# The loads of a decoder step's first ten microseconds dealt out anew over three queues, with four warm-up matmuls fewer

## What is computed

```python
h = RMSNorm(x)                        # x * rsqrt(mean(x*x) + eps) * attn_norm_w
[xin | Bg | Cg | q | k | v | g_conv | g_attn] = h @ w_in          # 1024 x 6400
y_conv = Bg * causal_depthwise_conv3(Cg * xin)
y_attn = sliding_window_attention(RMSNorm(q), RMSNorm(k), v)      # window 128, T5 bias, sinks
x = x + w_out(sigmoid(g_conv) * y_conv + sigmoid(g_attn) * y_attn)
x = x + MoE(RMSNorm(x))               # top 4 of 32 experts: 1024 -> 2 x 1024 -> 1024
```

## Time and profile before

| | |
|---|---|
| median of 3 runs | 1148.07 us (1147.94 to 1150.03) |
| the profiled execution: span from its first to its last instruction | 1145.4 us |
| TensorE busy | 1097.6 us, 96% of the span |
| mean granted TensorE clock | 0.993 |
| DVE, ACT, POOL busy | 38%, 16%, 8% |
| read from memory | 439.78 MB, 386 GB/s over the span |

### The profile page before, as it was taken

How to read it: one execution, slowest core, us unless ns; L and a number is a source line. 1 busy time by engine, 2 the same in 40 slices (tenths; PEclk the granted TensorE clock), 3 DMA queues, 4 the chain that set the end, 5 groups by cost and what they waited for, 6 DMA issues and landing times.

```text
span 1145.4 us, 15065 instructions
## 1 busy us (share of the span) xinstructions
PE 1097.6 (96%) x6055; PEld 497.1 (43%) x6055; DVE 437.5 (38%) x858; ACT 188.0 (16%) x398; POOL 88.4 (8%) x161
## 2 busy tenths in 40 slices
PE   9999999999999999999898999999999999999997
PEld 6689898543333333333333333333333333333332
DVE  4577786753433223233223232323232323232322
ACT  2133341221321101010101010101010101010101
POOL 1785215000000000000000000000000000000000
PEclk9999999999999999999999999999999999999999
DMA  9947629999999999999999999999999999999997
GB/s 313 314 128 186 210 85 353 416 357 425 400 420 426 419 432 431 430 433 431 433 433 429 434 430 433 435 428 434 429 434 431 431 434 429 435 429 434 425 423 287
DMA packets 53206, 444.36 MB, mean 388 GB/s; under 512 B 13101, under 2 KB 19373, under 8 KB 35741
## 3 DMA queue, kind: packets, MB, share of 16 engines
q1 hardware_dynamic: 46712, 435.83, 91.7%
q0 software_dynamic: 5600, 7.32, 2.4%
q10 hardware_dynamic: 852, 0.64, 0.2%
HBM read 439.78 MB, written 2.37 MB: 386 GB/s over the span
## 4 chain that ended last, share of the span: by engine, by line
PE 62%; DMA 37%; DVE 0%; issue 0%; ACT 0%; ACTq 0%; SPq 0%; DVEq 0%
PE pA L2051 32%; PE pB L2051 21%; DMA ring<-in_w_up 21%; DMA ring<-in_w_down 10%; PE pM L2051 6%; DMA area<-in_w_up 5%; PE pM L2054 1%; PE pA L2054 1%; DMA x<-in_x_prompt 1%; ACT area L1269 0%; DVE x L1898 0%; SPq L800 0%; DVE conv_row L1812 0%; DVE area L1973 0%; DVE x L1978 0%
## 5 line engine op out<-in xcount | busy, mean ns | idle before, releaser
L2051 PE MATMUL pA<-ring,hn 128*64 128x512 f32 x1536 | 352.6, 602 | 23.0 <-DMA ring<-in_w_up 23.0
L2051 PEld LDWEIGHTS pA<-ring,hn 128*64 128x64 f32 x1536 | 105.3, 137 | 218.8 <-issue 185.5
L2051 PE MATMUL pB<-ring,area 128*64 128x512 f32 (+2 forms) x784 | 171.5, 591 | 6.6 <-DMA ring<-in_w_down 5.8
L2051 PE MATMUL pA<-area,hn 128*64 128x512 f32 x512 | 119.3, 610 | 10.4 <-DMA area<-in_w_up 10.4
L2051 PE MATMUL pB<-area,ring 128*128 128x132 f32 (+2 forms) x928 | 126.4, 327 | 0.0
L2051 PEld LDWEIGHTS pB<-area,ring 128*128 128x128 f32 (+1 forms) x928 | 106.7, 175 | 18.2 <-issue 2.3
L2051 PEld LDWEIGHTS pB<-ring,area 128*64 128x64 f32 (+2 forms) x784 | 58.5, 136 | 101.2 <-issue 87.8
L1898 DVE TENSOR_TENSOR x<-pM,x 128x512 f32<-128x512 f32 x60 | 40.1, 691 | 147.7 <-PE pM L2051 147.7
L1257 ACT ACTIVATE area<-area 128x512 f32<-128x512 f32 x30 | 18.9, 631 | 385.2 <-DVE area L1881 385.2
L1812 DVE COPY conv_row<-pM 128x512 f32<-128x512 f32 x30 | 20.6, 686 | 146.0 <-PE pM L2051 146.0
L2051 PEld LDWEIGHTS pA<-area,hn 128*64 128x64 f32 x512 | 36.2, 139 | 74.5 <-issue 59.7
(11 more groups left out here) (348 smaller groups left out, 907.1 us busy)
## 6 DMA issues: line engine op xcount, KB each, us to landing
ring<-in_w_up SPq DMA_DIRECT2D x36, 4096.0 KB, 29.8
ring<-in_w_down SPq DMA_DIRECT2D x18, 4096.0 KB, 29.0
area<-in_w_up SPq DMA_DIRECT2D x12, 4096.0 KB, 30.2
ring<-in_w_up SPq DMA_DIRECT2D x16, 2048.0 KB, 13.4
area<-in_w_down SPq DMA_DIRECT2D x6, 4096.0 KB, 30.0
ring<-in_w_in SPq DMA_DIRECT2D x22, 1024.0 KB, 10.0
ring<-in_w_down SPq DMA_DIRECT2D x16, 1024.0 KB, 11.6
ring<-in_w_up SPq DMA_DIRECT2D x16, 1024.0 KB, 8.4
```

Of the source, the lines that this page charges most:

```text
L2051: return pe.matmul(out, w, m, start=start, stop=stop, skip_group_check=True)
```

## The change

Five things are rearranged, and none of the arithmetic changes:

1. ACT's queue issues `ident` and the norm weights first, then x10, then x11.
2. x01 is issued by GpSimd, as its first instruction after the block begins, and no longer by SP, so that chunk 0 of `w_in` moves up one place on SP's queue.
3. ACT squares x10 between `raw_columns(0)` and `raw_columns(1)`, no longer ahead of the sample rows.
4. DVE squares x00 ahead of the copy of the norm column, and x01 behind both scalings of the first block; the latter now ends with a wait of DVE for its own instruction.
5. `keep_busy` runs 8 matmuls instead of 12.

```diff
         @block.sync
             sp.dma_start(x[0:DEC, 2, :], x_sample.rearrange("b t d -> (b t) d")).then_inc(x_sample_loaded, 16)
-            sp.dma_start(x[:, 0, 512:D], x_prompt[0, 0:128, 512:D]).then_inc(x_loaded[0][1], 16)
             for n, (dst, src) in enumerate(w_in_chunk(0)):
         @block.gpsimd
         def _(pool):
+            pool.dma_start(x[:, 0, 512:D], x_prompt[0, 0:128, 512:D]).then_inc(x_loaded[0][1], 16)
             pool.wait_ge(cleared, 1)
         @block.scalar
         def _(act):
-            act.dma_start(x[:, 1, 0:512], x_prompt[0, 128:256, 0:512]).then_inc(x_loaded[1][0], 16)
             act.dma_start(ident, consts[:, C_ID:C_ID + 128]).then_inc(ident_loaded, 16)
             act.dma_start(rows[V_ANORM:V_ANORM + KT, :], attn_norm_w.rearrange("(k p) -> k p", p=128)).then_inc(anorm_loaded, 16)
+            act.dma_start(x[:, 1, 0:512], x_prompt[0, 128:256, 0:512]).then_inc(x_loaded[1][0], 16)
             act.dma_start(x[:, 1, 512:D], x_prompt[0, 128:256, 512:D]).then_inc(x_loaded[1][1], 16)
...
-            act.wait_ge(x_loaded[1][0], 16)
-            nc.scalar.activation(hn[:, 1, 0:512], x[:, 1, 0:512], ACT.Square, accum_out=stat[:, 1:2])
             act.wait_ge(x_sample_loaded, 16)
...
             raw_columns(0)
+            act.wait_ge(x_loaded[1][0], 16)
+            nc.scalar.activation(hn[:, 1, 0:512], x[:, 1, 0:512], ACT.Square, accum_out=stat[:, 1:2])
             raw_columns(1)
...
                 elif what == "anorm":
+                    squared(0)
                     V.tensor_copy(cols[:, V_ANORM:V_ANORM + KT], misc_bank()[:, 0:KT]).then_inc(misc_free, 1)
                     dve.wait_ge(misc_free, FILL["anorm", 0])
                 elif what == "s_cols":
                     weighted(0, KT, SEQ, DEC, misc_bank()[:, 0:KT * DEC]).then_inc(misc_free, 1)
-                    squared(0)
                     dve.wait_ge(x_halves, 1)
                     weighted(0, 4, 0, 128, pA[:, 0:512]).then_inc(raw_dve, 1)
-                    ins = squared(1)
                     dve.wait_ge(x_halves, 3)
                     weighted(4, 4, 0, 128, pA[:, 512:1024]).then_inc(raw_dve, 1)
+                    link(squared(1))
                     dve.wait_ge(raw_dve, 2)
...
-            keep_busy(zeros[:, 0:128], zeros, 12)
+            keep_busy(zeros[:, 0:128], zeros, 8)
```

## The result

The changed kernel takes 1149.9 us (median of 20 runs, 1148.62 to 1152.36) against 1147.95 us of the kernel before (20 runs, 1146.87 to 1150.03). The ratio is 1.0017, 95% interval 1.0011 to 1.0024. So the change costs some 2 us. That is within the 0.2% that I called the same, but on the other side of the forecast, and the interval does not reach 1.

A forecast was written before the change was run, and what follows sets the result against it. It took a chain 62% TensorE and 37% transfers to bound the kernel, with the k product's start waiting for x11. Sum: 1145.4 profiled - 0.4 + 2.67 (median over profile) = 1147.7 us; 8-in-10 range 1145.8 to 1150.3.

The forecast's parts named there:

- the term of x11: Opening: x11 lands at 9.0 us instead of 9.37, so the k product starts 0.4 us earlier.
- the holes: DMA engines not full while x11 waits, shares 0.74 and 0.40 from 3.6 to 6.0 us; filling them wins up to 1.03.
- my bad bound: Opening: first weights set out 0.39 us earlier and compete with x11, which lands up to 0.39 later.
- not at 6.6: Opening: x10, third on ACT's queue, lands at about 6.6 us, costed by x01's 4.8 on SP's queue.
- The second rival: Opening: x10 or x01 lands late and replaces x11 as last; k starts at 10.5, 1148.5 us in all; chance 0.12.
- The clock rival: TensorE's clock is low when the k product starts: 1.75 to 2.65 us more, 1149.5 us in all; chance 0.20.
- The sign that I named for it: K product: its 16 matmuls taking over 5 us instead of 3.56 would show TensorE's clock low.
- the 9.7 that I had named: Opening: predicted k product start in us; a clock rise after it would make the k product slow.
- Nothing by itself: Warm-up: four matmuls fewer free TensorE at 4.7 instead of 6.5 us, but gain nothing, as x11 comes last.
- my bounds: Opening: x01 from POOL takes 4.8 to 6.6 us plus 1.1, landing between 5.5 and 8.4; 7 taken.
- the 9.15 and 10.9: Opening: kv0 lands by 9.15 us and kv1 by 10.9, 0.39 earlier; neither sets the k product's start.
- The carry: From k product to kernel end: a start earlier or later by d moves the end by d, one to one.

The follow-up runs named there:

- e6: Kernel before with only x01 issued by GpSimd (POOL) instead of SP, 12 warm-up matmuls: ratio 1.0016.
- e10: Kernel before with x01 on GpSimd and three small row transfers put ahead of the first weights on SP's queue: ratio 1.0005.
- e15: Changed kernel with three small transfers put ahead of the first weights on SP's queue, x01 still on POOL, 8 warm-up matmuls: ratio 1.0002.
- e16: Changed kernel with three small transfers put ahead of the first weights on SP's queue, x01 still on POOL, 12 warm-up matmuls: ratio 1.0000.
- e4: Kernel before with only the identity and norm weights issued ahead of x10 on ACT's queue: ratio 1.0002.
- e5: Kernel before with only the warm-up cut from 12 matmuls to 8: ratio 1.0003.
- e7: Kernel before with only the new order of squares on ACT and DVE (parts 3 and 4 of the change): ratio 1.0001.
- e9: Kernel before without any warm-up matmuls: ratio 1.0011.
- e12: Changed kernel with x01 back on SP's queue ahead of the weights, 8 warm-up matmuls: ratio 1.0010.
- e13: Kernel before with six matmuls on zeros added between the last transposes and the k product: ratio 1.0009.
- e14: Changed kernel with x01 back on SP's queue ahead of the weights and 12 warm-up matmuls: ratio 1.0003.
- e1: Changed kernel with matmuls on zeros added on TensorE, 6 ahead of the turn of x10 and 3 ahead of x11: ratio 1.0011.
- e2: Changed kernel with 12 warm-up matmuls instead of 8: ratio 1.0007.
- e3: Changed kernel with x10 first again on ACT's queue, ahead of the identity and norm weights, 8 warm-up matmuls: ratio 1.0023.
- e11: Changed kernel with x11 behind the sample rows on SP's queue, then small rows, then weights; x01 on POOL; 10 warm-up matmuls: ratio 1.0001.
- e8: Kernel before with x10 on SP's queue, sample rows on ACT's, x01 and x11 on POOL's, the new order of squares, 12 warm-up matmuls: ratio 1.0001.

## Why the prediction was wrong

**The step that failed is the term of x11.** I took 0.4 us earlier, "since the holes are there in any case". The holes were filled, but mostly with the weights (0.60 MB instead of 0.30 between 3.6 and 7.2 us), and x11 came 0.43 later, just past my bad bound of 0.39. That bound counted only the 0.39 us by which the weights set out earlier. It left out that x01 had stood between them and the front of SP's queue: once it was gone, SP's queue ran weights against x10, the norm weights and x11 on ACT's, whichever was next there. e6 does it with one line (1.0016); e10, e15 and e16 undo it by holding the weights back, with x01 still on POOL (1.0005, 1.0002, 1.0000).

In 16 profiles x11 is the fourth transfer on ACT's queue. Its landings fall into three groups that do not touch:

| x01 | weights set out at | x11 lands at | ratios |
|---|---|---|---|
| SP (before, e4, e5, e7, e9, e12, e13, e14) | 2.0 | 8.04 to 9.37 | 1.0001 to 1.0003 (e4, e5, e7, e14); 1.0009 to 1.0011 with other warm-ups or fillers (e9, e12, e13) |
| POOL (changed, e1, e2, e3, e6) | 1.7 | 9.57 to 10.30 | 1.0007 to 1.0023 |
| POOL (e10, e15, e16) | 3.5 | 6.76 to 7.39 | 1.0000 to 1.0005 |

One thing these groups do not part: the weights were held back by 1.9 us, and the change had moved them by only 0.39. What x01 as a third queue costs with the weights at 2.0, if anything, no run shows.

**The size of the term was read from one execution.** Five profiles have x's loads as in the kernel before: x11 lands at 9.37, 8.36 (e5), 8.04 (e7), 9.14 (e9) and 8.42 (e13). The 7.05 us of the earlier trace rows is the slow end of a spread of 1.3 us. Three have the loads of the changed kernel: 9.80, 9.97 and 10.04. So between the medians of these, 8.42 and 9.97, the change moved x11 by about 1.5 us, not by the 0.43 that two single profiles show, and my 0.4 was a third of the spread. Not all of the 1.5 reaches k, since an early x11 leaves k to the warm-ups and the scaling (e7, 9.73).

**x10 lands at 7.79, not at 6.6.** It was costed by x01's 4.8 us on SP; on ACT's queue against the weights it took 6.0. The second rival had named this, with the right reason (x10 shares the engines with the weights) and 8.85 as its worst. It did not set the end here: TensorE waited 1.62 us for it and x11 still came last. The clock fell at 8.3, behind that wait.

**The clock rival holds for about half of the loss.** The sign that I named for it, 16 matmuls in over 5 us, did not come: they took 3.99. But transposes and k product lost 0.45 and 0.43. Of the 1.95 us between the medians of the runs, the late x11 with the clock up is worth about 0.8 (1.0007 in e2, and k at 10.74 there), and the rest goes with the clock, as far as the medians tell. That the total fell on the 1149.5 of this rival is in part luck: about half came from a late x11, which the rival did not have.

I gave it 0.20, with "work from 1.2 to about 6 stays almost unbroken" against it. That argument does not hold. In e15 TensorE has no gap from 1.2 us on, and its clock rose only at 9.4. The rise is the first clock record of a trace; ahead of it the column shows 1.00, but the matmuls run at the lower level. With 12 warm-ups it came between 4.0 and 7.1 us in all ten profiles. With 8 it came at 4.9 in the changed kernel's own profile, and at 9.2 (e12), 9.4 (e15), 9.5 (e5), 10.2 (e1) and 12.7 (e3) in the other five, two of them past the 9.7 that I had named. So the changed kernel's profile, in which the clock rose early, fell behind the wait for x10 and was back at 11.70, shows one execution's way to a slow k product and perhaps not the usual one. That the wait brought the clock down is not shown: in e2 waits of 1.24 and 1.18 us did not. Where the loads come early, the missing four matmuls give back what the slow clock takes: TensorE is free 1.7 us sooner (warm-up of 3.60 us against 5.30), and 16 transposes at the lower level take 1.6 us longer (3.60 in e15, 2.04 in e13). All pairs, 8 warm-ups against 12:

| | 8 | 12 |
|---|---|---|
| as in the change | 1.0017 | 1.0007 (e2) |
| x01 back on SP | 1.0010 (e12) | 1.0003 (e14) |
| weights held back | 1.0002 (e15) | 1.0000 (e16) |
| kernel before | 1.0003 (e5) | 1 |

The pairs differ by 0.0010, 0.0007, 0.0002 and 0.0003, all the same way, and more where transfers are late. No single pair separates by its intervals (each about 0.0009 to either side). That the missing four cost something where loads are late is likely, not shown. "Nothing by itself" fits where the loads come early (e5, e15), as the sum of gain and loss.

**What held.** x01 from POOL lands at 5.24, 4.0 us after its issue, quicker than my bounds (7.0 in e6 was within them). kv0 landed at 8.69 and kv1 at 10.62, within the 9.15 and 10.9. The new order of squares costs nothing that can be told (e7), nor does x10's place by itself (e4).

**The carry.** From 28 to 100 us the trace is late by the same 1.32 at every mark, as predicted. After that it is not exact: 0.61 came on top at SP's block moves. Over the 18 profiles the span grows with the start of the q product by 1.17 us per us (least squares, correlation 0.83), so a late opening is paid in full as far as this can tell, with some 0.8 us of scatter for a single run. Whether an early one is returned differs from case to case. At DVE's `conv_row<-pM` ahead of the experts (227.43 in the profile before) e11 is still 0.65 us early, e15 0.56 and e12 0.34, while e8 has lost its 0.64 at the block moves; at the last one (1068.71) e11 is 0.04 early, e15 0.37 and e12 0.42.

The Trainium skill ("DMA: Bandwidth & Descriptors", section "Issuing engines are not separate DMA queues") has it that transfers started by different engines interleave on the same 16 and that several issuers save issue time only. The trace agrees that they interleave (q0, q1 and q10 above in one stretch), but that is not all that counts: e6 moved one transfer to another issuer, let the weights move up by it, and lost 0.16%.

**Open:** why ACT's queue gets so little. In e6 the 16 engines are not full while it waits: the three shares above make 76% of the stretch. So it is not only that the weights use up the engines. What holds ACT's queue while the norm weights are under way is not shown, and no run takes that transfer away. Issued second, ahead of x10, they landed at 4.4 to 5.0 in all ten profiles that have them there. Also open is what makes SP's block moves slower at 101 us in some runs (12.1 us in e6 and 12.0 in e8, against 10.0 in e15 and 10.6 in e7); it doesn't go with the start of the opening, since e8 is early.

## What to carry to other kernels

Before a transfer is moved off a queue, look at what moves up behind it: if that is bulk which nobody needs yet, it can be served against the small transfers that everybody waits for, and idle DMA engines need not go to the transfer one has in mind. Hold the bulk back (here by three small transfers ahead of it, 1.0002 against 1.0017) before the urgent ones are spread over more queues, which gained nothing here. And profile the kernel before several times, or build neutral variants of it, before a term smaller than its landing times' own spread (here 1.3 us) is trusted.

## What the runs showed of the hardware

- A transfer of 4 KB in 8 rows, third on the same queue, landed between 3.3 and 6.1 us after its issue (issued at 1.68, landed at 5.00 in e5 and at 7.78 in e6). With all loads as in the kernel before, it landed anywhere from 5.00 (e5) to 6.84 (e9).
- 256 KB from POOL landed 4.0 us after the issue in the changed kernel, 4.3 in e15, 5.4 in e3 and 7.0 in e6, with nothing ahead of it on its queue; from SP, third on its queue, it took 4.8, and 3.5 (e4) to 5.4 (e9) in the others.
- With warm-up, TensorE's clock rose anywhere from 4.0 us (e2) to 7.1 (e4) with the same 12 matmuls, which then took 4.13 and 5.3 us; with 8 of them it rose between 4.9 (changed kernel) and 12.7 (e3). It can fall again before the first product: it was at 1.2 GHz from 8.30 to 11.70 in the changed kernel, after a stretch with TensorE half idle, and in e6 from 8.54 to 11.95.
